# Low halves for two k-tiles in one VectorE pass, and each k-tile's high-half products first on TensorE

## The chip, the cores and the metric

One core of one Trainium2 chip runs the whole program. The metric is device time in microseconds (us) of one execution; the median of three is quoted. TensorE does the matrix products, VectorE and ScalarE the elementwise work, SyncE and ScalarE issue transfers.

## The reference

A small decoder trunk, 256 tokens wide 2048 features, two layers and a final norm. Layer 0 has a token mixer (differential attention and retention), layer 1 a pooling mixer; each layer then has a gated feed-forward part with a causal convolution of width 3. That part is what the change is about:

```python
def conv_ffn(h, w_up, conv_w, conv_b, w_down):          # h 256 x 2048, w_up 2048 x 11264, w_down 5632 x 2048
    u = jnp.einsum('bsd,df->bsf', h, w_up)
    ...
        y = y + shifted * conv_w[CONV_WIDTH - 1 - tap]
    val, gate = jnp.split(y, 2, axis=-1)
    return jnp.einsum('bsf,fd->bsd', jax.nn.silu(gate) * val, w_down)
```

All of it is float32. The kernel reaches that accuracy with products of a rounded format: a weight tile and an activation tile are each split into a high half (the value rounded) and a low half (what rounding left), and three products are added: high by high, high activation by low weight, low activation by high weight.

## The kernel before

**Tiling.** A weight *unit* is 512 rows by 512 columns (1 MB), four *k-tiles* of 128 rows. Units are loaded by SyncE's queue into four raw slots (`raw`). For each k-tile ScalarE writes the high half `hi[:, kt]` (`w_hi`, L896), VectorE subtracts it from the raw weight and writes the low half `lo[:, kt]` (`w_lo`, L1309), and TensorE multiplies (`token_unit`, L654, L656, L657). `hi` and `lo` hold four k-tiles each, so ScalarE may write a k-tile only when TensorE is done with the k-tile four before it.

**Semaphores.** `hi_done` and `lo_done` count finished k-tiles, `w_used` counts k-tiles that TensorE is done with. `w_hi` waits for `w_used`, `w_lo` for `hi_done`, `token_unit` for `lo_done`. Each engine runs its program in the order in which it is written.

**The up loop.** The up-projection is 11 turns for each layer, the first written out (`peel`) and ten in a hardware loop. A turn makes 512 value and 512 gate features; I call each of these a *half-turn*: four units, 16 k-tiles, 96 matmuls. I name the k-tiles of a half-turn t0 to t15, and t-1 is the last of the half-turn before. Between its low halves VectorE does the previous half-turn's other work: after t3 it transposes the finished sums out of PSUM (`turn_up`, L1714), after t7 and t11 it adds convolution taps (`tap1`, `tap0`, L1733, L1741), after t15 it scales rows that came back by DMA (`scale_turned`, L1725). ScalarE does, between its high halves, `conv0` (L1101) after each of t0 to t3, whose first one waits for `scale_turned`. After t3 it waits for `turn_up` and issues the transfer of the transposed rows (`rows_away`, L1107); only then does it go on with t4.

**The down loop.** The down-projection is four groups of eleven units for each layer, with `token_unit` too, but for layer 0's last group (`wide_unit`, L540, L544) and layer 1's last three units (`tail_units`). Group 0 still carries the last half-turn's work: `conv0`, `turn_up` and `rows_away` in unit 0, `conv0` in unit 4, eight taps after unit 5. Groups 1 to 3 carry four times four small transposes (`turn_down`).

Of the kernel before, what the change touches and what calls it, by code (L numbers as in the profile page):

```python
# [23 lines left out]
ALU = mybir.AluOpType  # L24
ACT = mybir.ActivationFunctionType
AX = mybir.AxisListType
F32 = mybir.dt.float32
F32R = mybir.dt.float32r

P = 128  # L30
# [5 lines left out]
KT = 4  # L36


def trunk_kernel(nc, xT, rel_bias, norm_g, w_in, w_out, lam, subln, pool_w, pool_scale,
# [95 lines left out]
    with ctx:  # L135
# [191 lines left out]
        def tail_weights(i):  # L327

            if i == TAIL - 1:
                return hi, lo  # L330
            return h[:, 8 * i:8 * i + KT, :], h[:, 8 * i + KT:8 * i + 2 * KT, :]
# [197 lines left out]
        def _(pe):  # L529
# [115 lines left out]
            def token_unit(n, acc, first, last, j, ready=None, src=h, base=0):  # L645

                for kt in range(KT):
                    pe.wait_ge(lo_done, base + KT * n + kt + 1)
                    if ready is not None:
                        ready(kt)  # L650
                    for t in range(2):
                        xh = src[:, KT * j + kt, t * P:(t + 1) * P]
                        xl = src[:, KT * j + kt, S + t * P:S + (t + 1) * P]
                        pe.matmul(acc[:, t, :], xh, hi[:, kt, :], start=first and kt == 0, stop=False,  # L654
                                  skip_group_check=True)
                        pe.matmul(acc[:, t, :], xh, lo[:, kt, :], start=False, stop=False, skip_group_check=True)  # L656
                        mm = pe.matmul(acc[:, t, :], xl, hi[:, kt, :], start=False, stop=last and kt == KT - 1,  # L657
                                       skip_group_check=True)
                    mm.then_inc(w_used, 1)

# [643 lines left out]
        def _(ve):  # L1304
            def w_lo(n, base, slot, kts=range(KT), between=None, halves=(hi, lo)):

                for kt in kts:
                    ve.wait_ge(hi_done, base + KT * n + kt + 1)
                    ve.tensor_tensor(halves[1][:, kt, :], raw[:, slot, kt, :], halves[0][:, kt, :].bitcast(F32),  # L1309
                                     ALU.subtract).then_inc(lo_done, 1)  # L1310
                    if between is not None:
                        between(kt)

            def add_squares(n, g):

                ve.wait_ge(sq_ready, 4 * n + g + 1)
                if g > 1:
                    ve.wait_ge(sq_added, SQ_BASE[n] + g - 1)
                ve.tensor_tensor(sqacc[:, :, :], sqacc[:, :, :], sqt[:, :, :], ALU.add).then_inc(sq_added, 1)
# [456 lines left out]
            for l in range(DEPTH):  # L1776
# [21 lines left out]
                def v_windows(i, peel):  # L1798
                    q = i * 2 + (l * 2 * PAIRS - 1)
                    for j in range(UP_UNITS):  # L1800
                        between = None
                        if peel and l == 0 and j == 2:
                            between = lambda kt: h_lo_group(1, 3, 1, [kt])
                        if peel and l == 1:
                            between = lambda kt: h_lo_group(3, j, 3, [kt])
                        w_lo(U_UP[l] + j, i * (8 * KT), j, between=between)
                        if peel:
                            if l == 0 and j == 0:
                                add_mixed(3)
                            if l == 0 and j == 3:  # L1810
                                add_squares(1, 3)
                            if l == 1 and j == 0:
                                pool_out(1)
                                pool_out(2)
                            if l == 1 and j == 1:
                                pool_out(3)
                            if l == 1 and j >= 2:
                                add_squares(3, j - 1)
                            continue
                        if j == 0:  # L1820
                            turn_up(i * (8 * KT) + KT * U_UP[l], G_UP[l] - 1)
                        if j == 1:
                            tap1(i * 2 + (l * 2 * PAIRS - 2), i - 1, l, 0)
                        if j == 2:
                            tap0(i * 2 + (l * 2 * PAIRS - 2), i - 1, l, 0)
                        if j == 3:
                            scale_turned(q, i * 32 + (16 * (l * (2 * PAIRS - 1)) - 16))
# [11 lines left out]
                def g_windows(i):  # L1839
                    q = i * 2 + (l * 2 * PAIRS)  # L1840
                    for j in range(UP_UNITS):
                        last_taps = None
                        if j == 2:
                            last_taps = lambda kt: tap0(i * 2 + (l * 2 * PAIRS - 1), i - 1, l, 1, (2, 3)) if kt == 0 else None
                        w_lo(U_UP[l] + 4 + j, i * (8 * KT), j, between=last_taps)
                        if j == 0:
                            turn_up(i * (8 * KT) + KT * (U_UP[l] + 4), G_UP[l])
                        if j == 1:
# [31 lines left out]
                for g in range(1, DN_GROUPS):  # L1880
                    for j in range(DN_UNITS):
# [3 lines left out]
                        if j == 7 and l == 0:  # L1885
                            between = lambda kt: h_lo_group(2, g - 1, 2, [kt])
                        tail = l == 1 and g == DN_GROUPS - 1 and j >= DN_UNITS - TAIL
                        w_lo(U_DN[l] + DN_UNITS * g + j, 0, j % 4, between=between,
                             halves=tail_weights(j - (DN_UNITS - TAIL)) if tail else (hi, lo))
                        if j == 4:  # L1890
                            add_turned(l, g - 1)
                        if j == 8 and g > 1:
# [135 lines left out]
```

## Time and profile before

| | before |
|---|---|
| median of 3 runs | 1905.06 us (1905.02 to 1905.55) |
| profiled execution, its own time | 1905.34 us |
| span of its instructions | 1903.5 us |
| mean granted TensorE clock | 0.999 of full speed |
| busy: TensorE, VectorE, ScalarE | 1895.3, 1413.5, 1065.5 us |

The span runs from the first instruction to the last; 1.8 us of the profiled execution lie outside it. A matmul's row in the profile lasts longer than the distance to the next matmul, because matmuls overlap. So the distance from start to start says what one costs in a stream, and a short stall may hide inside "busy".

### The profile page before, as it was taken

Reading aid. Unit: us, or ns where it says so; the run is one execution under the profiler, and the core shown is the slowest. Engines: PE = TensorE matmul, PEld = TensorE weight load, DVE = VectorE, ACT = ScalarE, POOL = GpSimd, SP = SyncE. Lnnn points to the kernel's source line nnn. Section 1 sums busy time; section 2 is a strip of 40 time slices with the busy share of each in tenths; the row PEclk is TensorE's granted clock in tenths of the full one; section 3 lists DMA queues with packets and bytes.
Section 4 is the critical chain, followed back from the end, with each engine's and each line's share of the span. In section 5 each row is a group of like instructions: output and inputs, shape, how many; then the busy total and the mean of one; then the engine's idle time right before and its main releaser. Section 6 shows DMA issues by size and latency. Waiting matters only on the chain.

```text
span 1903.5 us, 26742 instructions
## 1 busy us (share of the span) xinstructions
PE 1895.3 (100%) x8630; PEld 1578.3 (83%) x8630; DVE 1413.5 (74%) x2324; ACT 1065.5 (56%) x1796; POOL 2.8 (0%) x6
## 2 busy tenths in 40 slices
PE   9999999999999999999999999999999999999998
PEld 8888888888888888888888888888888888888887
DVE  6767977777777777777766667777777777767665
ACT  7555545556555655556554557565555655555544
POOL 0000000000000000000000000000000000000000
PEclk9999999999999999999999999999999999999999
DMA  9776666666787777876665545677787777755653
GB/s 316 272 230 214 202 218 197 221 203 212 241 246 237 241 237 244 246 243 218 208 214 199 195 161 186 222 243 234 244 248 245 236 231 249 238 186 197 218 199 111
DMA packets 233664, 423.53 MB, mean 222 GB/s; under 512 B 14035, under 2 KB 54396, under 8 KB 233596
## 3 DMA queue, kind: packets, MB, share of 16 engines
q1 hardware_dynamic: 201484, 376.83, 61.4%
q10 hardware_dynamic: 32112, 45.81, 8.1%
q8 instruction: 41, 0.67, 0.1%
q14 instruction: 27, 0.22, 0.0%
HBM read 390.34 MB, written 30.68 MB: 221 GB/s over the span
## 4 chain that ended last, share of the span: by engine, by line
PE 99%; DMA 0%; ACT 0%; issue 0%; DVE 0%
PE ps L654 30%; PE ps L657 30%; PE ps L656 30%; PE ps L540 4%; PE ps L544 2%; PE ps L618 1%; PE ps L633 0%; PE ps L637 0%; PE ps L622 0%; PE ps L641 0%; PE ps L583 0%; PE ps L585 0%; PE ps L584 0%; PE ps L827 0%; PE ps L829 0%; PE ps L686 0%
## 5 line engine op out<-in xcount | busy, mean ns | idle before, releaser
L896 ACT ACTIVATE hi<-raw 128x512 fp32r<-128x512 f32 x1336 | 831.6, 630 | 763.3 <-PE ps L657 700.3
L1309 DVE TENSOR_TENSOR lo<-raw,hi 128x512 fp32r<-128x512 f32 x1352 | 911.2, 689 | 456.3 <-ACT hi L896 443.9
L654 PE MATMUL ps<-hi,h 128*128 128x512 f32 x1824 | 712.1, 390 | 0.0
L657 PE MATMUL ps<-hi,h 128*128 128x512 f32 x1824 | 709.9, 389 | 0.0
L656 PE MATMUL ps<-lo,h 128*128 128x512 f32 x1824 | 709.7, 389 | 0.0
L657 PEld LDWEIGHTS ps<-hi,h 128*128 128x128 f32 x1824 | 342.4, 188 | 71.7
L656 PEld LDWEIGHTS ps<-lo,h 128*128 128x128 f32 x1824 | 342.6, 188 | 70.3
L654 PEld LDWEIGHTS ps<-hi,h 128*128 128x128 f32 x1824 | 342.5, 188 | 70.1
L654 PE MATMUL ps<-hi,act 128*128 128x512 f32 x592 | 230.5, 389 | 0.0
L657 PE MATMUL ps<-hi,act 128*128 128x512 f32 x592 | 230.3, 389 | 0.0
L656 PE MATMUL ps<-lo,act 128*128 128x512 f32 x592 | 230.3, 389 | 0.0
L654 PEld LDWEIGHTS ps<-hi,act 128*128 128x128 f32 x592 | 111.1, 188 | 23.2 <-issue 0.5
L656 PEld LDWEIGHTS ps<-lo,act 128*128 128x128 f32 x592 | 111.1, 188 | 23.2
L657 PEld LDWEIGHTS ps<-hi,act 128*128 128x128 f32 x592 | 111.1, 188 | 23.1
L1101 ACT ACTIVATE yg<-u,cw 128x256 f32<-128x256 f32 x88 | 52.0, 591 | 17.9 <-DVE u L1725 17.9
L540 PE MATMUL ps<-act,hi 128*128 128x512 f32 x176 | 60.8, 394 | 0.0
L1101 ACT ACTIVATE yv<-u,cw 128x256 f32<-128x256 f32 x88 | 51.9, 590 | 14.5 <-DVE u L1725 14.5
L1725 DVE TENSOR_TENSOR u<-sqacc,rstd 128x512 f32<-128x512 f32 x84 | 54.1, 685 | 0.8 <-DMA sqacc<-turned_rows 0.8
L1714 DVE STREAM_TRANSPOSE sqt<-ps 128x1024 f32<-128x1024 f32 x42 | 52.2, 1243 | 0.0
L544 PE MATMUL ps<-act,lo 128*128 128x256 f32 x176 | 48.1, 277 | 0.0
L1760 DVE STREAM_TRANSPOSE u<-ps 32x256 f32<-32x256 f32 x96 | 42.8, 446 | 2.9
L540 PE MATMUL ps<-mixed,hi 128*128 128x512 f32 x128 | 43.9, 394 | 0.0
(210 smaller groups left out, 1107.2 us busy)
## 6 DMA issues: line engine op xcount, KB each, us to landing
raw<-in_w_up SPq DMA_DIRECT2D x176, 1024.0 KB, 5.7
raw<-in_w_down SPq DMA_DIRECT2D x88, 1024.0 KB, 5.1
raw<-in_w_in SPq DMA_DIRECT2D x52, 1024.0 KB, 5.5
turned_rows<-sqt ACTq DMA_DIRECT2D x42, 512.0 KB, 5.9
sqacc<-turned_rows ACTq DMA_DIRECT2D x168, 128.0 KB, 5.9
raw<-in_w_out SPq DMA_DIRECT2D x16, 1024.0 KB, 5.4
raw<-in_w_in SPq DMA_DIRECT2D x16, 256.0 KB, 5.4
row_store<-sqt SPq DMA_DIRECT2D x8, 512.0 KB, 3.0
```

Of the source, the lines that this page charges most:

```text
L540: pe.matmul(ps[:, bank + m, :], hi[:, kt, m * P:(m + 1) * P], mv, start=first and kt == 0, stop=False, skip_group_check=True)
L544: return pe.matmul(ps[:, bank + m, S:2 * S], lo[:, kt, m * P:(m + 1) * P], mv[:, 0:S], start=False, stop=last and kt == KT - 1, skip_group ...
L618: pe.matmul(acc[:, m, :], hi[:, kt, c], mv, start=first and kt == 0 and a == 0, stop=False, skip_group_check=True)
L654: pe.matmul(acc[:, t, :], xh, hi[:, kt, :], start=first and kt == 0, stop=False, skip_group_check=True)
L656: pe.matmul(acc[:, t, :], xh, lo[:, kt, :], start=False, stop=False, skip_group_check=True)
L657: mm = pe.matmul(acc[:, t, :], xl, hi[:, kt, :], start=False, stop=last and kt == KT - 1, skip_group_check=True)
L896: a_.activation(out[:, kt, :], raw[:, slot, kt, :], ACT.Copy).then_inc(hi_done, 1)
L1101: a_.activation(y[:, m, :], u[:, m, :], ACT.Identity, scale=cw[:, l, bass.ds(t, 1), 2], bias=cw[:, l, bass.ds(t, 1), 3]).then_inc(y0, 1)
L1309: ve.tensor_tensor(halves[1][:, kt, :], raw[:, slot, kt, :], halves[0][:, kt, :].bitcast(F32), ALU.subtract).then_inc(lo_done, 1)
L1714: ve.transpose(turned_u.rearrange("p (q k s) -> p q k s", q=4, k=8), rows).then_inc(evacuated, 1)
L1725: scaled = ve.tensor_tensor(out, quads, r, ALU.mult)
L1760: ve.transpose(cols, rows).then_inc(x_turned, 1)
```

## The change

Three edits. In `token_unit` (all its callers) TensorE waits for the k-tile's high half, does the four products that need only `hi`, then waits for the low half and does the two products with `lo`; before, one wait for `lo` stood ahead of all six. A new `w_lo_pairs` makes low halves for two k-tiles in one instruction of 128x1024, waits for the second one's high half, and adds 2 to `lo_done`. It takes the place of `w_lo` in the ten looped turns of each layer's up-projection (320 passes in both layers) and in down groups 1 to 3 (132). The first turn of each up-projection, down group 0 and everything ahead of the feed-forward parts keep `w_lo`.

```diff
@@ token_unit
                 for kt in range(KT):
-                    pe.wait_ge(lo_done, base + KT * n + kt + 1)
+                    pe.wait_ge(hi_done, base + KT * n + kt + 1)
...
+                    for half in range(2):
+                        for t in range(2):
+                            xt = src[:, KT * j + kt, half * S + t * P:half * S + (t + 1) * P]
+                            pe.matmul(acc[:, t, :], xt, hi[:, kt, :], start=first and kt == 0 and half == 0, stop=False,
+                                      skip_group_check=True)
+                    pe.wait_ge(lo_done, base + KT * n + kt + 1)
                     for t in range(2):
                         xh = src[:, KT * j + kt, t * P:(t + 1) * P]
-                        xl = src[:, KT * j + kt, S + t * P:S + (t + 1) * P]
-                        pe.matmul(acc[:, t, :], xh, hi[:, kt, :], start=first and kt == 0, stop=False,
-                                  skip_group_check=True)
-                        pe.matmul(acc[:, t, :], xh, lo[:, kt, :], start=False, stop=False, skip_group_check=True)
-                        mm = pe.matmul(acc[:, t, :], xl, hi[:, kt, :], start=False, stop=last and kt == KT - 1,
+                        mm = pe.matmul(acc[:, t, :], xh, lo[:, kt, :], start=False, stop=last and kt == KT - 1,
                                        skip_group_check=True)
                     mm.then_inc(w_used, 1)
@@ new, beside w_lo
+            def w_lo_pairs(n, base, slot, between=None, halves=(hi, lo)):
+
+                for kt in range(0, KT, 2):
+                    ve.wait_ge(hi_done, base + KT * n + kt + 2)
+                    ve.tensor_tensor(halves[1][:, kt:kt + 2, :], raw[:, slot, kt:kt + 2, :],
+                                     halves[0][:, kt:kt + 2, :].bitcast(F32), ALU.subtract).then_inc(lo_done, 2)
+                    if between is not None:
+                        between(kt)
+                        between(kt + 1)
@@ g_windows; v_windows (when not peel) and the down groups 1 to 3 likewise
-                        w_lo(U_UP[l] + 4 + j, i * (8 * KT), j, between=last_taps)
+                        w_lo_pairs(U_UP[l] + 4 + j, i * (8 * KT), j, between=last_taps)
```

TensorE in the up loop, one k-tile, before:

```order
L648 REGISTER_ALU
L654 MATMUL ps<-hi,h 128x512 [waits lo_done]
L656 MATMUL ps<-lo,h 128x512
L657 MATMUL ps<-hi,h 128x512
L654 MATMUL ps<-hi,h 128x512
L656 MATMUL ps<-lo,h 128x512
L657 MATMUL ps<-hi,h 128x512
```

and now:

```order
L648 REGISTER_ALU
L654 MATMUL ps<-hi,h 128x512 [waits hi_done]
L654 MATMUL ps<-hi,h 128x512 x3
L659 MATMUL ps<-lo,h 128x512 [waits lo_done]
L659 MATMUL ps<-lo,h 128x512
```

Six matmuls as before; the two with `lo` stand last and have a wait of their own, and one register instruction serves both waits.

VectorE in the up loop, from k-tile t2 to t5 of a gate half-turn, around `turn_up`, before:

```order
L1308 REGISTER_ALU
L1309 TENSOR_TENSOR lo<-raw,hi 128x512 [waits hi_done]
L1308 REGISTER_ALU
L1309 TENSOR_TENSOR lo<-raw,hi 128x512 [waits hi_done]
L1714 STREAM_TRANSPOSE sqt<-ps 128x1024 [waits w_used]
L1308 REGISTER_ALU
L1309 TENSOR_TENSOR lo<-raw,hi 128x512 [waits hi_done]
L1308 REGISTER_ALU
L1309 TENSOR_TENSOR lo<-raw,hi 128x512 [waits hi_done]
```

and now:

```order
L1319 REGISTER_ALU
L1320 TENSOR_TENSOR lo<-raw,hi 128x1024 [waits hi_done]
L1726 STREAM_TRANSPOSE sqt<-ps 128x1024 [waits w_used]
L1319 REGISTER_ALU
L1320 TENSOR_TENSOR lo<-raw,hi 128x1024 [waits hi_done]
```

The transpose stands behind a pass that cannot begin before t3's high half, and the pass behind it cannot begin before t5's.

## Rows read from the trace of the kernel before

**Rows 1.** The page: busy times, and the chain that ended last.

```profile
PE 1895.3 (100%) x8630; PEld 1578.3 (83%) x8630; DVE 1413.5 (74%) x2324; ACT 1065.5 (56%) x1796; POOL 2.8 (0%) x6
...
PE 99%; DMA 0%; ACT 0%; issue 0%; DVE 0%
```

**Rows 2.** Timeline of TensorE in a gate half-turn: start us, us, operation.

```profile
620.92 0.39 PE L654 MATMUL ps<-hi,h 128*128 128x512 f32 x1
...
626.36 0.39 PE L654 MATMUL ps<-hi,h 128*128 128x512 f32 x1
...
627.26 0.39 PE L656 MATMUL ps<-lo,h 128*128 128x512 f32 x1
```

**Rows 3.** The waits: engine line waited for, total us, times, longest us.

```profile
ACT hi L896 <- PE ps L657: 700.3, 917, 2.1
DVE lo L1309 <- ACT hi L896: 443.9, 732, 2.7
```

**Rows 4.** Timeline of TensorE in the program's first unit.

```profile
8.50 0.61 PE L633 MATMUL ps<-hi,h 128*128 128x512 f32 x2
...
9.86 0.39 PE L633 MATMUL ps<-hi,h 128*128 128x512 f32 x1
```

**Rows 5.** VectorE's groups by shape: count, busy us, mean ns, idle before.

```profile
L1309 DVE TENSOR_TENSOR lo<-raw,hi 128x512 fp32r<-128x512 f32 x1352 | 911.2, 689 | 456.3 <-ACT hi L896 443.9 <-ACT hi L999 4.2 <-ACT hi L1010 1.6
...
L1751 DVE TENSOR_TENSOR act<-yg,act 128x1024 fp32r<-128x1024 f32 x2 | 2.5, 1226 | 0.5 <-ACT act L1124 0.5
```

**Rows 6.** Timeline of VectorE, same half-turn; in brackets idle time and releaser.

```profile
616.34 0.69 DVE L1309 TENSOR_TENSOR lo<-raw,hi 128x512 fp32r<-128x512 f32 x1 [0.67 <-ACT hi L896]
616.95 1.29 DVE L1725 TENSOR_TENSOR u<-sqacc,rstd 128x512 f32<-128x512 f32 x2
...
621.78 0.69 DVE L1309 TENSOR_TENSOR lo<-raw,hi 128x512 fp32r<-128x512 f32 x1 [0.43 <-ACT hi L896]
622.39 1.24 DVE L1714 STREAM_TRANSPOSE sqt<-ps 128x1024 f32<-128x1024 f32 x1
624.80 1.90 DVE L1309 TENSOR_TENSOR lo<-raw,hi 128x512 fp32r<-128x512 f32 x3 [1.16 <-ACT hi L896]
```

**Rows 7.** Timeline of ScalarE, same half-turn.

```profile
617.04 0.63 ACT L896 ACTIVATE hi<-raw 128x512 fp32r<-128x512 f32 x1 [0.73 <-PE ps L657]
618.49 0.60 ACT L1101 ACTIVATE yg<-u,cw 128x256 f32<-128x256 f32 x1 [0.82 <-DVE u L1725]
619.00 0.62 ACT L896 ACTIVATE hi<-raw 128x512 fp32r<-128x512 f32 x1
...
620.53 0.59 ACT L1101 ACTIVATE yg<-u,cw 128x256 f32<-128x256 f32 x1
621.12 0.63 ACT L896 ACTIVATE hi<-raw 128x512 fp32r<-128x512 f32 x1
...
623.66 0.34 ACTq L1107 DMA_DIRECT2D turned_rows<-sqt  x1
624.13 1.70 ACT L896 ACTIVATE hi<-raw 128x512 fp32r<-128x512 f32 x3 [1.89 <-PE ps L657]
```

**Rows 8.** Timeline of the first unit, where TensorE waited for a low half.

```profile
6.72 0.69 DVE L1309 TENSOR_TENSOR lo<-raw,hi 128x512 fp32r<-128x512 f32 x1 [1.13 <-ACT hi L999]
...
7.47 0.73 PE L637 MATMUL ps<-lo,h 128*128 128x512 f32 x2
...
8.03 0.40 PE L641 MATMUL ps<-hi,h 128*128 128x512 f32 x1
```

**Rows 9.** Timeline of layer 0's down group 0, unit 6, the same wait.

```profile
935.63 1.88 DVE L1309 TENSOR_TENSOR lo<-raw,hi 128x512 fp32r<-128x512 f32 x3
...
936.21 0.39 PE L657 MATMUL ps<-hi,act 128*128 128x512 f32 x1
...
936.45 0.47 PE L654 MATMUL ps<-hi,act 128*128 128x512 f32 x1
...
936.76 0.40 PE L656 MATMUL ps<-lo,act 128*128 128x512 f32 x1
```

More of the change, by code:

```diff
@@ L1805, in v_windows @@
                             between = lambda kt: h_lo_group(3, j, 3, [kt])
-                        w_lo(U_UP[l] + j, i * (8 * KT), j, between=between)
+                        if peel:
+                            w_lo(U_UP[l] + j, i * (8 * KT), j, between=between)
+                        else:
+                            w_lo_pairs(U_UP[l] + j, i * (8 * KT), j, between=between)
                         if peel:
@@ L1887, in _ @@
                         tail = l == 1 and g == DN_GROUPS - 1 and j >= DN_UNITS - TAIL
-                        w_lo(U_DN[l] + DN_UNITS * g + j, 0, j % 4, between=between,
-                             halves=tail_weights(j - (DN_UNITS - TAIL)) if tail else (hi, lo))
+                        w_lo_pairs(U_DN[l] + DN_UNITS * g + j, 0, j % 4, between=between,
+                                   halves=tail_weights(j - (DN_UNITS - TAIL)) if tail else (hi, lo))
                         if j == 4:
```

## The prediction

> **What bounds the kernel now.** I read the page first. TensorE is busy 1895.3 us of a span of 1903.5 and makes 99% of the chain that ended last [rows 1]. Busy time hides short stalls, so I read its timeline next. In a half-turn of the up loop k-tile t0 starts at 620.92 and t4 at 626.36 [rows 2]: 5.44 us for four k-tiles of six matmuls, 1.36 us a k-tile, 0.2267 us a matmul. Thus the stream has no stall here, and the same distance holds all through both up loops. The waits then show who is slack: ScalarE waits 700.3 us in sum for TensorE to free high halves, VectorE 443.9 us for ScalarE [rows 3]. Nothing in the loops waits on VectorE. So what the change saves there is worth nothing in itself; the time can only move if the distance between matmuls changes, or if a half now arrives too late. The second needs the margins, which I take from the timelines of VectorE and ScalarE beside TensorE's.
>
> **Order of the matmuls.** The same six matmuls, in the order high, high, high, high, low, low, with consecutive ones going to alternate accumulators. The program's first unit already has such an order (pairs that alternate): its k-tile starts at 8.50 and the next at 9.86 [rows 4], again 1.36 us. I cost the new order at nothing. The second wait adds no instruction, since it rides on a weight load and uses the same register; met early, it costs nothing, as in that first unit.
>
> What it gives is time: a low half is wanted four matmuls later, at 0.91 us into the k-tile. But hardly any k-tile is late before, so this is credit and no gain. The small gain: once in each layer, in down group 0 after eight taps, a low half is late and costs 0.09 us (the rows are given below), which the credit removes: -0.2 us in all.
>
> **The pass over two k-tiles.** No 128x1024 subtraction into `lo` exists before. The nearest row, the same operation at that shape into the same format, takes 1226 ns; one k-tile takes 689 ns [rows 5]. I take 1.22. It must wait for the second k-tile's high half, so each pair ends 1.22 us after that half, where the last single one ended 0.69 after: 0.53 us later. In a row of back-to-back passes the start distance counts: three passes take 1.90 us [rows 6], hence 0.605 apart, two of them 1.21, and a pair some 1.22 - 0.09 = 1.13 (the next operation starts 0.09 before the end). That is 0.08 us saved for each of 452 pairs, 36 us of VectorE time, all off the path.
>
> The Trainium skill (VectorE: DVE Perf Modes, "The TRN2 errata — SBUF-src ops pay a fixed extra latency per instruction") says that one large operation pays the fixed latency once and that float32 adds take (N+151)/0.96 ns. That gives 691 and 1224 ns, and the rows agree within 2 ns; by it 452 pairs save 0.157 us each, 71 us, and on the path still nothing.
>
> **Where 0.53 us matters.** I follow one half-turn, TensorE's k-tiles held where they are. Before: the low half of t-1 starts at 616.34 and the scaling ends at 616.95 + 1.29 = 618.24 [rows 6]; `conv0` starts at 618.49, 0.25 later, and the high half of t1 at 619.00 [rows 7]. Now:
>
> 1. The pair (t-2, t-1) runs 616.34 to 617.56. Scaling ends 0.53 later, 618.77, and `conv0` starts at 619.02.
> 2. High half of t1: 619.53 to 620.15. Pair (t0, t1): 620.18 to 621.40. Its first use is at 620.92 + 0.91 = 621.83: 0.43 to spare.
> 3. ScalarE alternates `conv0` and high halves 0.51 apart (619.00 to 620.53 is three steps [rows 7]), so t3's high half, which began at 621.12, now begins at 621.56 and ends at 622.19. The slip is 0.44, since before it was held a little by TensorE.
> 4. Pair (t2, t3): 622.22 to 623.44. Before, t3's low half ended at 621.78 + 0.69 = 622.47.
> 5. `turn_up` started at 622.39 and now starts at 623.35: 0.96 late. It ends at 624.59 in place of 623.63.
> 6. ScalarE is queued behind it: `rows_away` went at 623.66 and t4's high half at 624.13; three high halves take 1.70 [rows 7], so t5's ended at 624.13 + 0.535 + 0.63 = 625.30. Now 626.26.
> 7. Before, t4 needed only its own low half: 624.80 + 0.69 = 625.49, 0.87 ahead of 626.36. Now the pair (t4, t5) waits for t5: 626.29 to 627.51. The first `lo` matmul of t4 is due at 626.36 + 0.91 = 627.27. **It is 0.24 us late.**
>
> The credit of 0.91 is eaten by 0.96 (the transpose's slip), 0.51 (waiting for t5's high half: it ended at 625.30, VectorE began at 624.80) and 0.53 (the longer pass) against a margin of 0.87.
>
> A late low half costs more than its lateness. In the first unit the low half ended at 6.72 + 0.69 = 7.41, the waiting matmul started at 7.47, 0.06 after, and its pair took 0.56 in place of 0.453, 0.11 more [rows 8]. In the down loop the low half ended at 936.32, the matmul started at 936.45, 0.13 after, and the next came at 0.31 in place of 0.227, 0.08 more [rows 9]. So the price is 0.24 + 0.06 + 0.11 = 0.41 to 0.24 + 0.13 + 0.08 = 0.45; with 0.03 for rounding in the rows, 0.38 to 0.48. I take 0.44.
>
> After the stall ScalarE and VectorE catch up: from t6 on the high halves are again held by TensorE, and the next half-turn begins as in step 1, so the stall repeats. A value half-turn has one more VectorE pass (1.22) before t0, which still ends before t1's high half; steps 2 to 7 are the same.
>
> **How often.** 20 looped half-turns in each layer. The first has its scaling in a unit that keeps single passes, two k-tiles earlier, so steps 1 and 3 slip nothing: the transpose is 0.5 late and the pair just in time. 19 remain in each layer, 38 in all. In down group 0, `turn_up` stands between single passes: step 1's slip reaches t3 but not step 4's, nor the pair's wait, so no stall. In groups 1 to 3 only small work stands between pairs (small transposes and single additions of 128x1024, 1.2 us at most), which the 1.5 us that a pair leaves free of each 2.72 us takes up. An unhindered high half ends 3.25 us before its k-tile (617.04 + 0.63 = 617.67 against 620.92 [rows 2, 7]), so a pair ends 3.25 - 1.36 - 0.03 - 1.22 = 0.64 before the first of its two. That is 1.55 ahead of the first `lo` matmul, and 0.64 in layer 0's last group, which keeps the wait in front. Without that cover each pair there would cost what it is late. The transfers of raw tiles are issued 0.5 us later, with slots four units deep; no wait on them shows in [rows 3].
>
> **The sum.** 38 x 0.44 = 16.7, less 0.2: +16.5 us on the profiled execution's 1905.34, which lies 0.3 above the median of 1905.06. On the median: 1921.6. With 0.38 and 0.48: 1919.3 and 1923.1.
>
> **Rivals.**
> - *No stall, hence no change.* If t5's high half comes, or the pair ends, 0.37 us sooner than I worked out, the wait is met in time. Then the time is 1904.9, no change. For it: the chain has seven steps and ends only 0.24 late. Against: each step is a row or a sum of two. A lesser slip gives something between. Chance 0.13.
> - *Faster.* The alternate accumulators, or `hi` streamed four times running, shorten the distance between matmuls. Each ns off the distance is 7.4 us on 7440 such matmuls, so against stalls of 16.5 it takes 3 ns of the 226.7 to be faster by over 0.2%. Against: [rows 4] have 226.7 in that very order. Chance 0.05; 1895 or so.
> - *Two stalls in each half-turn.* The pair (t0, t1) has 0.43 to spare, 0.3 after the delay of 0.06 to 0.13. If ScalarE's start slips by 0.3 more, t0 stalls as well, and the later stall stays: some 0.3 more for each, 38 x 0.74 = 28, so 1933. Chance 0.08.
> - *The clock.* Short stalls might lower TensorE's granted clock; it is 0.999 now. At the lower of its two levels, 1.2 GHz in place of 2.4, a distance of 0.227 becomes up to 0.45 us; a tenth of the up loops' 3840 matmuls there makes some 85 us, so 2005. The stalls in [rows 8, 9] are as long and are not followed by slower matmuls, so 0.02. The Trainium skill (TensorE: Matmul & The Clock Gate, "A second HAM failure mode: psum-queue depth-cycling") has kernels in which short idling between groups of matmuls kept re-throttling the clock; by that rule this rival would be the outcome, and the trace so far does not bear it out.
>
> **The numbers.** The forecast has 0.72, and alone would span 1916 to 1926. The range takes in part of a lesser slip and of the second stall: 1911 to 1930. Within 0.2% (3.8 us, about what a measurement of this kernel can tell) lies the rival without a stall: 0.13. Faster 0.05. Slower 0.82.
>
> **What the profile after would show.** TensorE waiting on VectorE's `lo` once in each half-turn, at the first `lo` matmul of t4, nowhere else; k-tile t4 at 1.8 us, the others at 1.36; a half-turn of 22.2 us in place of 21.76; `turn_up` some 0.5 us later against TensorE than before, once the stall is in; passes of 1.22 us; VectorE's busy time lower by 36 us (passes back to back) to 69 (2 x 0.689 - 1.226 for each pair, passes apart). I am wrong if k-tiles stay at 1.36 all through (no stall), if their distance differs everywhere (the order of matmuls matters), or if a second k-tile is long.

## The result and the profile after

| | before | after |
|---|---|---|
| median of 4 runs each, same session | 1905.24 us (1905.02 to 1905.55) | 1931.93 us (1931.50 to 1932.11) |
| ratio to before, 95% interval | | 1.0139 (1.0127 to 1.0151) |
| profiled execution, span | 1905.34, 1903.5 us | 1932.11, 1930.3 us |
| mean granted TensorE clock | 0.999 | 1.000 |

The change made the kernel 26.7 us slower. The prediction had 16.5 us more and a range that ended at 1930: the direction and the mechanism were right, the size was not.

The page of the kernel after: busy times, the chain that ended last by engine, and two groups (busy us, mean ns; idle time before and its releaser). The first two answer to [rows 1], the third to [rows 5].

```profile
PE 1908.1 (99%) x8630; PEld 1575.1 (82%) x8630; DVE 1364.1 (71%) x1872; ACT 1056.0 (55%) x1796; POOL 2.8 (0%) x6
...
PE 80%; DVE 6%; issue 5%; ACT 5%; DMA 2%; ACTq 1%; DVEq 0%
...
L1320 DVE TENSOR_TENSOR lo<-raw,hi 128x1024 fp32r<-128x1024 f32 x448 | 545.4, 1225 | 379.4 <-ACT hi L898 379.0
...
L659 PE MATMUL ps<-lo,h 128*128 128x512 f32 x1824 | 566.6, 392 | 14.1 <-DVE lo L1320 14.0
```

VectorE is busy 49.4 us less than before and the time is longer. The double pass takes 1225 ns. TensorE has now idled for VectorE's low halves, and the chain that ended last is no longer TensorE from end to end: it steps over to VectorE and ScalarE.

The waits of the kernel after: engine and line, what it waited for, total us, times, longest us. They answer to [rows 3].

```profile
ACT hi L898 <- PE ps L659: 705.1, 870, 2.5
DVE lo L1320 <- ACT hi L898: 379.0, 357, 2.4
...
PEld ps L659 <- DVE lo L1320: 31.0, 41, 1.1
...
PE ps L659 <- DVE lo L1320: 14.0, 38, 0.7
```

The last row did not exist before. It counts 38, one for each looped half-turn but the first of each layer, and all 38 are at k-tile t4. What it holds, 14.0 us, is only part of the price: a matmul's row lasts longer than the distance to the next one, so a stall in the distance is longer than the idle time that shows. The distances give the rest. Over every two matmuls of 512 columns that follow each other I summed what the distance has above 0.227 us. Distances of 0.25 us and more: 3.2 us before, 27.2 after. Distances of 0.229 to 0.25: 1.5 before, 3.3 after. Together that is 25.9 us more, of 26.8 that the span grew.

Now one half-turn, from t-1 to t6. VectorE's timeline of the kernel after (start us, us, operation; in brackets idle time before and its releaser). It is a value half-turn, with one more pass (L1763) than that of [rows 6].

```profile
642.61 1.23 DVE L1320 TENSOR_TENSOR lo<-raw,hi 128x1024 fp32r<-128x1024 f32 x1 [1.50 <-ACT hi L898]
643.75 1.29 DVE L1737 TENSOR_TENSOR u<-sqacc,rstd 128x512 f32<-128x512 f32 x2
...
646.53 1.23 DVE L1320 TENSOR_TENSOR lo<-raw,hi 128x1024 fp32r<-128x1024 f32 x1 [0.36 <-ACT hi L898]
648.56 1.23 DVE L1320 TENSOR_TENSOR lo<-raw,hi 128x1024 fp32r<-128x1024 f32 x1 [0.80 <-ACT hi L898]
649.70 1.24 DVE L1726 STREAM_TRANSPOSE sqt<-ps 128x1024 f32<-128x1024 f32 x1
652.70 2.36 DVE L1320 TENSOR_TENSOR lo<-raw,hi 128x1024 fp32r<-128x1024 f32 x2 [1.75 <-ACT hi L898]
```

ScalarE's, the same stretch; it answers to [rows 7].

```profile
645.81 0.62 ACT L898 ACTIVATE hi<-raw 128x512 fp32r<-128x512 f32 x1
...
647.84 0.62 ACT L898 ACTIVATE hi<-raw 128x512 fp32r<-128x512 f32 x1
...
650.98 0.34 ACTq L1109 DMA_DIRECT2D turned_rows<-sqt  x1
651.44 2.20 ACT L898 ACTIVATE hi<-raw 128x512 fp32r<-128x512 f32 x4 [2.49 <-PE ps L659]
```

And TensorE's at k-tile t4, which answers to [rows 2].

```profile
652.59 1.07 PE L654 MATMUL ps<-hi,h 128*128 128x512 f32 x4
653.98 0.73 PE L659 MATMUL ps<-lo,h 128*128 128x512 f32 x2 [0.32 <-DVE lo L1320]
654.55 1.08 PE L654 MATMUL ps<-hi,h 128*128 128x512 f32 x4
```

Read them from the end. t4 starts at 652.59, so its first `lo` matmul, the fifth of the k-tile, is due at 652.59 + 0.91 = 653.50. The pair (t4, t5) runs 652.70 to 653.93, and the matmul starts at 653.98: 0.48 late. Its pair of matmuls takes 0.57 in place of 0.453, another 0.11. So this stall costs 0.59, where the prediction had 0.44. The other distances are as they were: the k-tile is 1.96 us long, the next 1.37.

Then compare starts with ends. The high half of t3 ends at 647.84 + 0.62 = 648.46 and the pair starts at 648.56, 0.10 later. Of t1: 645.81 + 0.62 = 646.43, pair at 646.53, 0.10. Of t5, the second of the four: 652.60, pair at 652.70, 0.10. In the kernel before that distance was 0.03: ScalarE's high half of t-1 in [rows 6]'s half-turn ends at 615.68 + 0.63 = 616.31, and the low half starts at 616.34. Its row:

```profile
615.68 0.63 ACT L896 ACTIVATE hi<-raw 128x512 fp32r<-128x512 f32 x1 [0.73 <-PE ps L657]
```

The prediction used 0.03 for the pair. It is the first difference that needs an explanation.

The place is not t4 in every case. Once, early in layer 0's loop, the first `lo` matmul of t0 is late too. The scaling and TensorE there:

```profile
509.27 1.29 DVE L1737 TENSOR_TENSOR u<-sqacc,rstd 128x512 f32<-128x512 f32 x2 [0.31 <-DMA sqacc<-turned_rows]
```

```profile
512.25 1.07 PE L654 MATMUL ps<-hi,h 128*128 128x512 f32 x4
513.34 0.73 PE L659 MATMUL ps<-lo,h 128*128 128x512 f32 x2
```

The `lo` matmul was due at 513.16 and starts at 513.34, 0.18 late, and the next is 0.11 late. The scaling ahead of it had waited 0.31 us for rows that come back by DMA. Experiment 7 returns to this.

### The profile page after: what moved, and what is told of

It reads as the page before. It is cut to its first block, busy times and chain, and to the rows that moved or that the text cites. A ratio compares the mean times of both kernels' runs of the same rounds, so it can differ in the third digit from the quotient of the medians.

```text
span 1930.3 us, 26422 instructions
## 1 busy us (share of the span) xinstructions
PE 1908.1 (99%) x8630; PEld 1575.1 (82%) x8630; DVE 1364.1 (71%) x1872; ACT 1056.0 (55%) x1796; POOL 2.8 (0%) x6
## 4 chain that ended last, share of the span: by engine, by line
PE 80%; DVE 6%; issue 5%; ACT 5%; DMA 2%; ACTq 1%; DVEq 0%
PE ps L654 45%; PE ps L659 24%; PE ps L540 4%; ACT hi L898 4%; DVE lo L1320 3%; PE ps L544 2%; DMA sqacc<-turned_rows 2%; DVE sqt L1726 2%; DVE u L1737 2%; PE ps L618 1%; ACT yg L1103 1%; ACTq L1109 0%; PE ps L633 0%; PE ps L622 0%; PE ps L637 0%
## 5 line engine op out<-in xcount | busy, mean ns | idle before, releaser
L654 PE MATMUL ps<-hi,h 128*128 128x512 f32 x3648 | 979.2, 390 | 0.0
L1320 DVE TENSOR_TENSOR lo<-raw,hi 128x1024 fp32r<-128x1024 f32 x448 | 545.4, 1225 | 379.4 <-ACT hi L898 379.0
L659 PE MATMUL ps<-lo,h 128*128 128x512 f32 x1824 | 566.6, 392 | 14.1 <-DVE lo L1320 14.0
L1311 DVE TENSOR_TENSOR lo<-raw,hi 128x512 fp32r<-128x512 f32 x456 | 309.2, 687 | 156.3 <-ACT hi L898 148.8
L654 PE MATMUL ps<-hi,act 128*128 128x512 f32 x1184 | 316.4, 389 | 0.0
L659 PE MATMUL ps<-lo,act 128*128 128x512 f32 x592 | 182.3, 389 | 0.0
L540 PEld LDWEIGHTS ps<-act,hi 128*128 128x128 f32 x176 | 32.8, 188 | 7.9 <-issue 0.3
L1753 DVE SCALAR_TENSOR_TENSOR yg<-u,cw,yg 128x254 f32<-128x254 f32 x88 | 38.2, 478 | 0.0
L1745 DVE SCALAR_TENSOR_TENSOR yg<-u,cw,yg 128x255 f32<-128x255 f32 x88 | 36.6, 479 | 0.0
```

The costliest lines, as they stand in the source:

```text
L540: pe.matmul(ps[:, bank + m, :], hi[:, kt, m * P:(m + 1) * P], mv, start=first and kt == 0, stop=False, skip_group_check=True)
L654: pe.matmul(acc[:, t, :], xt, hi[:, kt, :], start=first and kt == 0 and half == 0, stop=False, skip_group_check=True)
L659: mm = pe.matmul(acc[:, t, :], xh, lo[:, kt, :], start=False, stop=last and kt == KT - 1, skip_group_check=True)
L1320: ve.tensor_tensor(halves[1][:, kt:kt + 2, :], raw[:, slot, kt:kt + 2, :], halves[0][:, kt:kt + 2, :].bitcast(F32), ALU.subtract).then_inc ...
L1753: ve.scalar_tensor_tensor(y[:, m, 2:S], u[:, m, 0:S - 2], cw[:, l, bass.ds(t, 1), 0], y[:, m, 2:S], ALU.mult, ALU.add).then_inc(y2, 1)
```

## The experiments

Each ratio is to the kernel before, measured in the same session; its median there was 1905.28 to 1905.34 us. The diffs are excerpts, against the kernel after.

**1. The order alone.** All low halves in single passes as before, TensorE's new order kept (at all three call sites):

```diff
-                            w_lo_pairs(U_UP[l] + j, i * (8 * KT), j, between=between)
+                            w_lo(U_UP[l] + j, i * (8 * KT), j, between=between)
...
```

> The new order of TensorE's matmuls and its second wait stay; every low half is again a single pass of one k-tile. My theory: the order is free, so the time is that of the kernel before, 1904.9 us (1904.3 to 1905.5), every k-tile of the loops at 1.36 us and no wait on a low half. Rival: part of the 26.7 us lost belongs to the order or to the second wait; then it is above 1907, and k-tiles are longer all through.

Measured: 1905.12 us (1904.72 to 1905.87), ratio 0.9999 (0.9990 to 1.0008). The order costs nothing and gives nothing. All 26.7 us are the passes'.

**2. The pairs alone.** The passes over two k-tiles, TensorE's old order with one wait in front of each k-tile:

```diff
-                    pe.wait_ge(hi_done, base + KT * n + kt + 1)
+                    pe.wait_ge(lo_done, base + KT * n + kt + 1)
...
-                    pe.wait_ge(lo_done, base + KT * n + kt + 1)
```

> Double passes with the old order on TensorE, one wait for the low half ahead of all six matmuls. My theory: without the 0.91 us of credit both t0 and t4 stall in each half-turn, by 0.67 and 0.11 more each (the second shorter by what the first gave back), 3.1 us a turn: 1961 to 1970 us. Rival: the wait in the middle of a k-tile is what costs, and a wait at its start is cheaper; then no more than the changed kernel's 1932.

Measured: 1969.17 us (1968.99 to 1969.61), ratio 1.0335 (1.0319 to 1.0350). The waits of that kernel:

```profile
PE ps L654 <- DVE lo L1318: 38.7, 78, 0.8
```

78 stalls: 40 at t4, one in each looped half-turn, and 38 at t0. The distances in front of the late matmuls are 0.80 to 0.93 us, but for two early ones of 1.1 to 1.2. The order's credit of 0.91 is real, and in the kernel after it covers t0 (all but once) and falls short at t4.

**3. Where the semaphore's count matters.** The double pass adds 2 to `lo_done`. In the trace's records of the kernel after, each of the 452 passes is preceded by a VectorE instruction of its own that holds the wait for `hi_done`, and the pass has none (the list of VectorE's instructions ahead of the prediction shows the wait on the pass); in the kernel before, the wait stands on the pass. Here a second semaphore counts k-tile pairs, so that the pass adds 1; all who waited for these k-tiles wait for half the number. The order of work is that of the kernel after; TensorE's wait for the low half in the loops has a register of its own.

```diff
+        lo_two = sem("lo_two")
...
-                                     halves[0][:, kt:kt + 2, :].bitcast(F32), ALU.subtract).then_inc(lo_done, 2)
+                                     halves[0][:, kt:kt + 2, :].bitcast(F32), ALU.subtract).then_inc(lo_two, 1)
```

> The changed kernel, with a second semaphore that counts passes by one, so that the double pass adds 1 and not 2. Everything else stays; TensorE's low-half wait in the loops gets a register of its own. My theory: adding 2 moves the pass's wait into an instruction of its own, and so each double pass starts 0.10 us after the high half and not 0.03; three such starts lie in the chain to t4. With 1 the wait rides on the pass again, the pass starts 0.03 after, the first waiting matmul is 0.30 late in place of 0.48 to 0.62, and the time is 1920 to 1922 us. Rival: a 128x1024 pass starts 0.07 later because of its size, however it counts; then nothing changes, 1932.

Measured: 1922.43 us (1922.07 to 1923.14), ratio 1.0091 (1.0075 to 1.0106). ScalarE's high half of t3 and VectorE's pair behind it, in that kernel:

```profile
646.45 0.62 ACT L916 ACTIVATE hi<-raw 128x512 fp32r<-128x512 f32 x1
```

```profile
647.10 1.23 DVE L1342 TENSOR_TENSOR lo<-raw,hi 128x1024 fp32r<-128x1024 f32 x1 [0.80 <-ACT hi L916]
```

The distance is 0.03 again (647.07 to 647.10). The first `lo` matmul of t4, TensorE's timeline:

```profile
651.24 1.07 PE L671 MATMUL ps<-hi,h 128*128 128x512 f32 x4
652.45 0.73 PE L676 MATMUL ps<-lo,h 128*128 128x512 f32 x2
```

It was due at 652.15 and starts at 652.45, 0.30 late, which is the prediction's 0.24 + 0.06; the next adds 0.11. 38 x 0.41 = 15.6, and small distances and the rest bring some 1.2 more, to the 16.8 us that the span is longer than in the kernel before. So over a third of the loss, 9.5 us, came from a bookkeeping detail: how much one instruction adds to a semaphore.

**4. Is it the count, or the size?** The kernel of experiment 1, with single passes, but each adds 2 to `lo_done`, and all waits on it are doubled:

```diff
-                                      ALU.subtract).then_inc(lo_done, 1)
+                                      ALU.subtract).then_inc(lo_done, 2)
```

> Single passes everywhere with TensorE's new order, and each pass adds 2 to its semaphore (all waits on it are doubled). My theory: every pass of 128x512 that waits now starts 0.10 us after its high half and not 0.03, so the late start comes of the count and not of the size; margins in the loops are 0.87 and more ahead of a use that is 0.91 later, so no stall there: 1905 to 1906.5 us, the first unit some tenths longer. Rival: 0.10 belongs to 128x1024; then singles still start at 0.03.

Measured: 1905.18 us (1904.57 to 1905.64), ratio 0.9997 (0.9988 to 1.0006). ScalarE's and VectorE's timelines there:

```profile
618.58 0.61 ACT L898 ACTIVATE hi<-raw 128x512 fp32r<-128x512 f32 x1
```

```profile
619.30 0.69 DVE L1311 TENSOR_TENSOR lo<-raw,hi 128x512 fp32r<-128x512 f32 x1 [0.88 <-ACT hi L898]
```

From 619.19 to 619.30 it is 0.11; over all such waits the median is 102 ns, against 33 before. So the pass's size is not the cause, the count is. It costs no time here, as single passes have margin. The other half is experiment 3, where passes of 128x1024 that add 1 start 33 ns after, in the median too.

**5. The transpose ahead of the pair.** Passes over two k-tiles counted as in the kernel after; `turn_up` stands behind the pair (t0, t1) in place of (t2, t3), in both kinds of half-turn:

```diff
+                            last_taps = lambda kt: turn_up(i * (8 * KT) + KT * (U_UP[l] + 4), G_UP[l]) if kt == 1 else None
                         w_lo_pairs(U_UP[l] + 4 + j, i * (8 * KT), j, between=last_taps)
-                        if j == 0:
-                            turn_up(i * (8 * KT) + KT * (U_UP[l] + 4), G_UP[l])
```

> The changed kernel with the transpose moved one pass ahead in both half-turns: behind the pair (t0, t1) and no longer behind (t2, t3). My theory: the stall comes of ScalarE being queued behind that transpose; moved, the rows go away at 1.8 us into the half-turn in place of 3.9, the high halves of t4 and t5 come over 1 us sooner, and no stall is left: 1904.5 to 1906.5 us with all 452 double passes. Rival: the double pass is too late in itself (its wait for the second high half); then 1920 or more stays.

Measured: 1906.15 us (1905.54 to 1906.78), ratio 1.0005 (0.9995 to 1.0014). VectorE's timeline:

```profile
642.59 1.23 DVE L1320 TENSOR_TENSOR lo<-raw,hi 128x1024 fp32r<-128x1024 f32 x1 [0.36 <-ACT hi L898]
643.73 1.24 DVE L1726 STREAM_TRANSPOSE sqt<-ps 128x1024 f32<-128x1024 f32 x1
644.89 1.18 DVE L1320 TENSOR_TENSOR lo<-raw,hi 128x1024 fp32r<-128x1024 f32 x1
646.85 1.23 DVE L1320 TENSOR_TENSOR lo<-raw,hi 128x1024 fp32r<-128x1024 f32 x1 [0.78 <-ACT hi L898]
```

The transpose fills time in which VectorE would wait for t3's high half, so `rows_away` and ScalarE's high halves behind it are not late. No row of TensorE waiting for `lo` is left. So the loss needs the transpose's place in the chain: with it gone, all 452 double passes, each with its late start, cost 0.9 us in the median, which the interval doesn't tell from nothing.

**6. Both mends.** Experiments 3 and 5 together.

> Double passes counted by one on their own semaphore, and the transpose one pass ahead. My theory: no stall, and without the separate waits the small rest that the run with the transpose ahead kept (0.9 us) shrinks: 1905.0 to 1905.8 us, the same as before, with VectorE's busy time 49 us lower. Rival: the saved VectorE time is worth something once nothing is late; then below 1904.

Measured: 1905.49 us (1904.97 to 1906.67), ratio 1.0001 (0.9992 to 1.0010). Its busy times:

```profile
PE 1895.8 (100%) x8630; PEld 1579.0 (83%) x8630; DVE 1360.9 (71%) x1872; ACT 1070.9 (56%) x1796; POOL 2.8 (0%) x6
```

VectorE works 52.6 us less than in the kernel before, and the time is the same. What the passes save is worth nothing here: TensorE has no wait that it could shorten.

**7. Single passes where the stall is.** Unit 1 of each looped half-turn (t4 to t7), value and gate, keeps single passes; the rest as in the kernel after:

```diff
-                        w_lo_pairs(U_UP[l] + 4 + j, i * (8 * KT), j, between=last_taps)
+                        (w_lo if j == 1 else w_lo_pairs)(U_UP[l] + 4 + j, i * (8 * KT), j, between=last_taps)
```

> The changed kernel with single passes for t4 to t7 of each looped half-turn, double ones elsewhere. My theory: the transpose stays 1.1 us late, but t4's low half no longer waits for t5's high half (0.5) nor takes 1.22 (0.53 more), so it ends some 0.7 us before its first use: no stall, 1904.5 to 1906.5 us. Rival: the late transpose alone is enough for a stall, since it holds ScalarE; then 1910 or more.

Measured: 1909.66 us (1906.77 to 1914.71), ratio 1.0023 (1.0014 to 1.0033). A miss: I expected no loss. The stall at t4 is gone, as it should be, but others came at t0, in ten half-turns of this profile (its execution took 1911.76 us). They are irregular, 0.1 to 1.1 us each. One of them, VectorE's timeline:

```profile
487.76 1.29 DVE L1737 TENSOR_TENSOR u<-sqacc,rstd 128x512 f32<-128x512 f32 x2 [1.08 <-DMA sqacc<-turned_rows]
490.53 1.22 DVE L1320 TENSOR_TENSOR lo<-raw,hi 128x1024 fp32r<-128x1024 f32 x1 [1.48 <-ACT hi L898]
```

and TensorE's:

```profile
489.96 1.07 PE L654 MATMUL ps<-hi,h 128*128 128x512 f32 x4
491.81 0.73 PE L659 MATMUL ps<-lo,h 128*128 128x512 f32 x2 [0.78 <-DVE lo L1320]
```

The rows that go out by `rows_away` come back by `sqacc<-turned_rows`. Here the scaling waited 1.08 us for them; `conv0`, t1's high half and the pair (t0, t1) are behind it, and its first matmul, due at 490.87, starts 0.94 late. In sum, who released the scaling in that kernel, from the view of its line:

```profile
  DMA sqacc<-turned_rows: 6.2, 9
```

Each of the ten t0 stalls has such a wait of the scaling ahead of it (the tenth is of 0.09 us). Of the distances of 0.25 us and more in the two loops all are at t0, and they hold 6.2 us above 0.227, of the 6.4 that this span is longer than before. So in this profile the returning rows are nearly the whole loss.

The time between the last returned row and the scaling's start (median) tells why this shows here and hardly elsewhere: 1.84 us in the kernel before, 1.91 in the kernel after, 0.60 here, 3.07 in experiment 5. From the issue of `rows_away` to the scaling the kernel after has 15.20 us and this kernel 14.56 (medians of the looped half-turns): the 0.6 of the stall at t4 lay between the two. The return itself, from its first issue to the last landing, took 7.36 us there and 7.96 here; why it took longer no run shows. Take the stall away without moving the transpose forward, and the transfers are next.

**8. Single passes in the last unit.** The edit of experiment 7 with `j == 3` (t12 to t15) in place of `j == 1`, so that the scaling isn't late by a longer pass:

> The changed kernel with single passes for t12 to t15 of each looped half-turn, so that the scaling and the first convolution pass go at their old time, and t4 keeps its double pass. My theory: the slip of steps 1 to 3 (0.5) goes, the transpose is 0.55 to 0.6 late in place of 1.1, and the pair (t4, t5) ends 6.29 us into the half-turn against 6.35: just in time in layer 0 (0 to 0.13 lost a half-turn), some 0.25 lost in the half-turns of layer 1 whose pass starts 0.12 later still: 1906 to 1910 us. Rival: the scaling's slip doesn't reach the transpose, because ScalarE has slack after t0; then the stall stays at 0.6 and the time above 1925.

Measured: 1911.01 us (1910.63 to 1912.42), ratio 1.0028 (1.0018 to 1.0039), 1 us above what I gave it, so a miss by its range. TensorE's timeline at t4:

```profile
650.25 1.07 PE L654 MATMUL ps<-hi,h 128*128 128x512 f32 x4
651.16 0.73 PE L659 MATMUL ps<-lo,h 128*128 128x512 f32 x2
651.73 1.09 PE L654 MATMUL ps<-hi,h 128*128 128x512 f32 x4
```

The first `lo` matmul is on time (651.16, due 651.16) and yet its pair takes 0.57 in place of 0.453. So the 0.11 is paid as soon as the wait is met at the last moment, in all 40 looped half-turns: 40 x 0.11 = 4.4 us of the 5.7, and with 0.03 of small distances each half-turn is 0.14 longer, 5.6 in all. The profiled execution (1911.90 us) has one larger stall, 0.85 at a t0, again behind a scaling that waited for its rows. The experiment also shows that the 0.53 of the first step counts in the chain: the 0.45 measured, less 0.44 for the slip and 0.07 for that pair's own start, puts the pass's end 0.06 before the matmul is due. VectorE's timeline there has it:

```profile
649.88 2.53 DVE L1320 TENSOR_TENSOR lo<-raw,hi 128x1024 fp32r<-128x1024 f32 x2 [1.75 <-ACT hi L898]
```

The pair (t4, t5) starts at 649.88 and takes 1.23, so it ends at 651.11, 0.05 before 651.16. The further 0.12 that I expected in layer 1 did not come.

**9. Experiment 7 with an earlier return.** All four return transfers issued at t9 in place of two at t9 and one each at t10 and t11:

```diff
-                for q in ((), (0, 1), (2,), (3,))[kt]:
+                for q in ((), (0, 1, 2, 3), (), ())[kt]:
```

> The kernel with single passes for t4 to t7 (1909.7 us, stalls of about 1 us in eight half-turns) with one more edit: ScalarE issues all four transfers of the returning rows after t9's high half, where it issued two, then one after t10's and one after t11's. My theory: with the stall at t4 gone, the late transpose leaves the rows' way out and back with 0.6 us to spare in the median in place of 1.8, and a straggling packet holds the scaling and so t0's low half. All four at once bring the last rows back about a microsecond sooner: no or hardly any big stall, 1905.5 to 1907.5 us. Rival: it is the way out that is late, or ScalarE's own queue; then the big stalls stay and the time is 1908 or more.

Measured: 1910.84 us (1908.76 to 1912.81), ratio 1.0028 (1.0017 to 1.0039). A miss. The scaling's waits for the transfers fell from 9 to 1 and the margin went from 0.60 to 1.42 us, but the time did not fall. From the same view of its line:

```profile
  DMA sqacc<-turned_rows: 0.9, 1
```

The distances tell why. At t0 those of 0.25 us and more now hold 0.9 us above 0.227, where experiment 7 had 6.2. But 2.4 us stand at t10, in twelve half-turns, where experiment 7 has none. ScalarE, VectorE and TensorE in one of them:

```profile
1340.27 2.40 ACTq L1118 DMA_DIRECT2D sqacc<-turned_rows  x4
1342.78 1.15 ACT L898 ACTIVATE hi<-raw 128x512 fp32r<-128x512 f32 x2 [3.44 <-PE ps L659]
```

```profile
1344.04 1.23 DVE L1320 TENSOR_TENSOR lo<-raw,hi 128x1024 fp32r<-128x1024 f32 x1 [1.84 <-ACT hi L898]
```

```profile
1343.95 1.07 PE L654 MATMUL ps<-hi,h 128*128 128x512 f32 x4
1345.32 0.73 PE L659 MATMUL ps<-lo,h 128*128 128x512 f32 x2 [0.30 <-DVE lo L1320]
```

The four issues stand in ScalarE's program ahead of the high halves of t10 and t11, and these begin only at 1342.78. The pair (t10, t11) ends at 1345.27, and the first `lo` matmul of t10, due at 1344.86, starts at 1345.32, 0.46 late. So the edit took the stalls at t0 away and made new ones at t10: the rival "ScalarE's own queue" in a form that the edit itself brought in. Such a pair ends 0.30 us before its use in the median here, 1.27 in experiment 7.

**10. Experiment 7 counted by one.** With the semaphore of experiment 3:

> The same kernel with single passes for t4 to t7, the transfers as before, but passes counted by one on their own semaphore. My theory: the transpose is some 0.15 to 0.2 us less late (two starts at 0.03 in place of 0.10), so the rows' return has 0.8 us to spare in the median; fewer half-turns stall: 1906 to 1909 us. Rival: the big stalls have nothing to do with how late the transpose is; then as many stay and the time is that of the run before, 1909.7.

Measured: 1909.01 us (1908.47 to 1910.89), ratio 1.0021 (1.0011 to 1.0031), at the edge of what I gave it. Its margin before the scaling is 1.05 us. In its profile (1908.64 us) three half-turns stall at t0, all early in layer 0's loop, with the late matmuls at 491.42, 514.08 and 536.68. Each has a scaling ahead of it that waited for returning rows, and no other scaling waited. They hold 1.5 us, smaller stalls at t4 of the same half-turns 0.5, and small distances all over the program 1.2, together 3.2 of the 3.3 that the span is longer than before. So the returning rows explain the large stalls of experiment 7 and their number goes with the margin: ten at 0.60, three at 1.05, two at 1.42 (experiment 9). In the medians that saved little (1909.66 and 1909.01), and each kernel has one profile only. Why the returns take longer in some half-turns, and why these kernels differ by several us from run to run, stays open.

## Why the prediction was off

- **The order costs nothing**: right (experiment 1), and its credit of 0.91 us is what turns 78 stalls of 0.7 to 0.8 us, the next matmul's share counted, into 38 of 0.6 (experiment 2). Down group 0, given 0.2 us for both layers, is 0.28 shorter.
- **VectorE's saving is off the path**: right. Busy time fell 49.4 us, within the 36 to 69 given, and experiment 6 shows it worth nothing.
- **Place and count**: right. One stall in each half-turn, at the first `lo` matmul of t4, 38 in all; the first half-turn of each layer is just in time, as predicted, and pays the next matmul's 0.11 even so. All others in the loops are in time but one t0. k-tile t4 is 1.96 us, where 1.8 was predicted, and two half-turns take 44.80 us in place of 43.52.
- **The chain of steps 1 to 7**: right in its members. Taking away the transpose's place in it ended the stall (experiment 5), taking away the longer pass of step 1 left it just in time (experiment 8), taking away the pair (t4, t5) itself ended it too (experiment 7). `turn_up`, predicted at 623.35 with t4 at 626.36, stands at 649.70 - 652.59 + 626.36 = 623.47.
- **The start of each pair**: this is the step that failed. Steps 2, 4 and 7 start the pair 0.03 us after the high half, a distance read from single passes that add 1; step 1 takes the old start outright. It is 0.10, because the pass adds 2. Three pairs stand in the chain, (t-2, t-1), (t2, t3) and (t4, t5), so 0.21 us in all: the term "0.24 us late" should have been 0.45, and the row above shows 0.43 at the pass's end. Experiment 3 gives the 0.07 back at each and lands on 0.24, and its 1922.43 us is within 1 us of the forecast of 1921.6, in part by luck: a stall there costs 0.41 and not 0.44, and the small distances make up for it. Experiment 4 shows that the count of 2 alone brings it.
- **The price of a late low half**: 0.06 to start and 0.11 on the next matmul, as in [rows 8]. Right. The second price, 0.13 to start from [rows 9], was misread: the matmul before it starts at 936.21, so this one was due at 936.44 and starts at 936.45, just about on time. Only the 0.08 behind it was a cost. In experiment 2, where the wait in front of the k-tile is really late, the matmul starts 0.05 us after the low half's end (median of 78). Without it the price is 0.41 us, where the sum took 0.44.
- **Not in the sum**: small distances of 0.229 to 0.25 us, 1.9 us more over the two loops. 1.3 of it is at t5 and t6, behind the stall, and 0.5 at t0 and t1, where experiment 5, which has no stall, has it too. And in nine of layer 1's ten gate half-turns a further 0.12, in the first of the ten 0.35. In the nine the pair begins 0.22 after the high half. ScalarE and VectorE in one of them, in the kernel after:

```profile
1482.37 2.19 ACT L898 ACTIVATE hi<-raw 128x512 fp32r<-128x512 f32 x4 [2.49 <-PE ps L659]
```

```profile
1483.74 2.36 DVE L1320 TENSOR_TENSOR lo<-raw,hi 128x1024 fp32r<-128x1024 f32 x2 [1.87 <-ACT hi L898]
```

t5's high half ends at 1483.52, the pair starts at 1483.74. With the wait on the pass (experiment 3) it does not occur. It isn't tied to layer 1: in experiments 7 and 9 the same 0.22 stands in layer 0's value half-turns, at the pair (t10, t11), and none in layer 1's loop, and in experiment 8, with separate waits too, neither loop has it. That the pass isn't ready to go when its separate wait ends is my guess; no run shows why some half-turns have it.
- **The sum again**, with measured terms, from the start of the n-th matmul in both kernels' traces. The up loops grew by 12.9 us in layer 0 and 13.9 in layer 1, 26.8 in all, as much as the span. Of the 38 stalled half-turns 27 grew by 0.65 (the stall of 0.59 and 0.06 of small distances), 17.6; nine of layer 1's gate half-turns by 0.76, 6.9; the first stalled one of layer 1 by 0.99, and the one of layer 0 that also stalls at t0 by 1.05; the first half-turns of both loops by 0.13 and 0.15. That makes 26.8. Outside the loops the differences cancel: -0.6 at the program's start, which other kernels' profiles have from -0.5 to +0.4, -0.3 in the two down groups 0, and +0.9 in layer 0's last down group, which is the next point.
- **Down groups 1 to 3**: the prediction had no stall there, with small work of 1.2 us at most between two pairs. There is one, once in the program, in layer 0's last group. VectorE and TensorE there, in the kernel after:

```profile
1119.95 0.94 DVE L1772 STREAM_TRANSPOSE u<-ps 32x256 f32<-32x256 f32 x2
1120.93 1.23 DVE L1778 TENSOR_TENSOR x<-u,x 128x1024 f32<-128x1024 f32 x1
1122.07 1.22 DVE L1320 TENSOR_TENSOR lo<-raw,hi 128x1024 fp32r<-128x1024 f32 x1
```

```profile
1123.44 0.47 PE L540 MATMUL ps<-act,hi 128*128 128x512 f32 x1
```

The small work between the two pairs is 2.1 us, two transposes and an addition. The pair ends at 1123.29, and the matmul, due at 1123.31, starts 0.13 late, the next 0.07. All nine kernels with double passes there, the kernel after among them, lose 0.13 to 0.21 us at this k-tile, the two without (experiments 1 and 4) nothing. In the same group the distances behind it are a little longer, 0.66 us in sum here and 0.68 in experiment 6, 0.04 or less in the other profiles; why, no run shows.
- **Rivals**: the clock stayed at its higher level, 2.4 GHz (a granted clock of 1.000 in the kernel after, with 38 stalls, and 0.999 in experiment 2, with 78). By the Trainium skill (TensorE: Matmul & The Clock Gate, "A second HAM failure mode: psum-queue depth-cycling") such regular idling could have re-throttled it; in no run here did the clock fall. The two-stall rival (1933) came near in time but not in kind: t0 stalls once in the kernel after, not 38 times.
- **Transfers**: the prediction looked at the transfers of raw tiles alone and left out the rows that return, on which the scaling waits. Two such waits stand in the kernel before (0.8 us in all, view of the waits), which cost TensorE nothing, and one in the kernel after, ahead of its stall at t0. In the median the rows had 1.84 us to spare. That is enough in the kernel after, but not in one in which the stall at t4 is taken away alone (experiment 7).

## What to carry to other kernels

When two small passes become one, look at three things before the saved engine time: what waits for the last input of the longer pass, what is queued behind it on its engine and on the next, and whether the merged instruction now adds more than 1 to a semaphore, since that alone moved each start by 0.07 us here, and three such starts in one chain, repeated 38 times, made 9.5 of the 26.7 us (with the 0.12 of layer 1's gate half-turns). A stall that is taken away gives back its time only up to the next late thing, here a transfer's return that the stall itself had covered. And when a mend brings no gain though the wait that it aimed at is gone, look where the stalls are now: in experiment 9 they had moved from t0 to t10.

## What the hardware showed unexpectedly

- A pass whose completion adds 2 to a semaphore starts 102 ns after the high half that it waits for, one that adds 1 starts 33 ns after (medians; at 128x512 experiment 4 against the kernel before, at 128x1024 the kernel after against experiment 3). In the records the first has its wait in a separate instruction.
- Behind such a separate wait, some starts came another 0.12 us late, one in each turn of one loop: layer 1's gate half-turns in the kernel after and experiments 2 and 5, layer 0's value half-turns in experiments 7 and 9, none in experiment 8.
- A `lo` matmul that is released at the last moment starts on time, but the next is 0.11 us late (experiment 8: 0.57 for the two in place of 0.453). So such a wait costs before it is late at all.
